# Fourteen seven-product pairs in rows in the last block, with weight sums made by adding transfers

## The chip, the cores and the metric

The program runs on one core of one Trainium2 chip. The metric is the device time of one launch in microseconds (us), as the median of several runs. The engines are TensorE (PE; PEld is its weight load), VectorE (DVE), ScalarE (ACT), GpSimd (POOL) and SyncE (SP), which issues the loads.

## What is computed

The reference chains a Mamba2 layer, a convolutional gated FFN, a differential attention layer, a second such FFN, and a mixed block that ends in a SwiGLU FFN, for 512 positions and a model width of 1024, all in float32. The change touches the code of the three FFNs; what matters most is the last one:

```
def swiglu(xn, w_gate, w_up, w_down):
    return (jax.nn.silu(xn @ w_gate) * (xn @ w_up)) @ w_down
...
D_FF = 2816        # 22 chunks of 128 features
```

The two FFNs before it have the same sizes, with a three-tap causal convolution between the product and the SiLU.

## The kernel before

**Layout.** Activations are kept feature-major: a chunk is 128 features on the partitions and 512 positions along the row. A float32 product is made of three passes of a rounded format (fp32r): each operand is split into a high part (ScalarE, a copy that rounds) and a low part (VectorE, a subtraction, called `cut`), and TensorE multiplies low by high, high by low and high by high.

**Plan.** A class `Plan` lays out the whole program ahead of time in ticks. A tick is one `Piece` of TensorE work: two chunks of contraction of a plain feature (6 matmuls of 512 columns) or one product of a seven-product pair (12 matmuls of 256 columns). Each engine's program then walks the ticks in order and issues what the plan has for that tick or for so many ticks earlier (`at("quad", T - age)`); real time is kept by semaphores alone, so an engine runs ahead until a wait holds it, and what stands behind the wait in its queue waits too.

**Weights.** They arrive by `load` on SyncE's queue into three raw buffers of 128x1024. A "unit" is one 128x1024 block (or less) that ScalarE splits and VectorE cuts into one of three high/low buffer pairs; `ring` schedules a unit's split two units ahead of its use and the cut `cut_age` ticks later. `load(r + 3)` waits until raw buffer `r` has been cut (and, for the pairs below, summed).

**The last FFN.** The gate and up features of chunk f (22 of each) share the input `n2`. A plain pair is two plain features: 48 matmuls of 512 columns in 8 ticks. Eleven of the 22 pairs (`QUADS` = 4, 5, 7, 8, 10, 12, 13, 15, 16, 18, 19) go by Strassen's scheme instead (`quad`): the 8 x 8 blocks (two halves of the positions, two halves of the contraction, gate and up) take seven products of 256 columns, 84 matmuls in 7 ticks. The products are formed in the order `PRODUCTS` in three banks, and their sums are finished from the banks by ScalarE copies and VectorE additions (`quads` in both programs). Sums of the inputs (`tees`) are made once. Sums of the weights are made per pair by VectorE from the two raw buffers: `sum1` and `sum2`, four additions of 128x512 into `s1` and `s2`. The gating product (`fmul`) of plain pairs runs on GpSimd, that of seven-product pairs on VectorE (`fmul_last`). No more than two such pairs stand in a row, and a plain pair stands between. `dn` are the down projections, after f = 11 and f = 21.

**Lines.** L1272 is every matmul, L1276 every transpose, L2230 VectorE's `tensor_tensor`, L2233 its `scalar_tensor_tensor`, L1715 ScalarE's copy, L1718 its other functions, L2877 GpSimd's `tensor_tensor`, L3027 the weight load on SyncE.

Of the kernel before, what the change touches and what calls it, by code (L numbers as in the profile page):

```python
# [9 lines left out]
F = mybir.dt.float32  # L10
# [143 lines left out]
QUADS = (4, 5, 7, 8, 10, 12, 13, 15, 16, 18, 19)  # L154
PRODUCTS = ("p1", "p2", "p6", "p5", "p7", "p3", "p4")
QUAD_BANK = {"p1": "b", "p2": "a", "p6": "b", "p5": "d", "p7": "b", "p3": "d", "p4": "b"}
QUAD_LAST = {"a": "p2", "d": "p3", "b": "p4"}
FIRST_ROW = 13
DIFF_ORDER = "k0 q0 k1 q1 v0 k2 q2 v1 k3 q3 k4 q4 v2 k5 q5 k6 q6 k7 q7 v3"


class Plan:
    def __init__(self):
        self.T = 0
        self.pieces = []
        self.units, self.unit_end, self.loads, self.quad_units = [], {}, [], {}
# [128 lines left out]
    def quad(self, f, gate, gate_c, up, up_c):  # L295

        key = ("gu", 2, f)
        self.until(lambda: self.past("tees", 3, 6) and self.place(
            [((*key, "b"), 0, 10), ((*key, "a"), 1, 4), ((*key, "d"), 3, 6)]), key)
        t = self.T  # L300
        self.loads += [(gate, 0, DC, gate_c + f * P, P), (up, 0, DC, up_c + f * P, P)]
        r = len(self.loads) - 2
        g = Group(key, False, "n2", 0, [], DC, 0, P, H2)
        sources = (("raw", r, 0, UNIT), ("s1", f, 0, UNIT), ("s2", f, 0, UNIT), ("raw", r + 1, S, S))
        for i, product in enumerate(PRODUCTS):
            if i % 2 == 0:
                age, self.cut_age = self.cut_age, 1 if i == 4 else self.cut_age
                u = self.ring(sources[i // 2])
                self.cut_age = age
                g.units.append(u)  # L310
            self.put(Piece(g, i // 2, i, i + 1, i == 0))
        self.quad_units[f] = (r, *g.units)
        for u, end in zip(g.units, (("bank", (*key, "a")), ("product", (f, "p5")), ("bank", (*key, "d")),
                                    ("bank", (*key, "b")))):
            self.unit_end[u] = end
        self.start("sum1", f, t - 5)
        self.start("sum2", f, t - 3)
        self.start("quad", f, t)
        src, i = h_of(2, f)
        self.lo[src, i] = t + 11  # L320
# [206 lines left out]
    def ffn(self, s, src, nxt, gate, gate_c, up, up_c, down, norm):  # L527
        late = 5 if s < 2 else 2
        if s == 2:
            for k in range(4):  # L530
                self.once("tees", k, lambda k=k: self.past("rms", "n2", 3) and (k == 0 or self.past("tees", k - 1, 4)))
        self.start("ffn", s)
        for h, (f0, nf) in enumerate(((0, 12), (12, 10))):
            def lo(h=h, f0=f0, nf=nf):
                for f in range(f0, f0 + nf):
                    t = self.ev.get(("up", s, f))
                    if t is not None:
                        self.lo[f"H{s}{h}", f - f0] = t + late

            self.rules.append(lo)  # L540
            for f in range(f0, f0 + nf):
                if s == 2 and f in QUADS:
                    self.quad(f, gate, gate_c, up, up_c)
# [285 lines left out]
class Waits:  # L829
# [23 lines left out]
    "tee_d", "tee_n1", "tee_t2", "tee_t", "tee_hi", "tee_lo", "sum1", "sum", "product", "q_copy", "q_row", "q_up", "q_read",  # L853
# [13 lines left out]
class Signals:  # L867
    def __init__(self, nc, ctx, known):
# [8 lines left out]
        self.tb2 = [Dma(sem(f"tb2{i}")) for i in range(4)]  # L877
        self.spill, self.mem, self.out = (Dma(sem(n)) for n in ("spill", "mem", "out"))
# [10 lines left out]
class Buffers:  # L889


    def __init__(self, nc, ctx):
# [41 lines left out]
        self.teeh, self.teel = (t[:, :, :].rearrange("p (i c) (h n) -> p i (c h) n", i=4, h=2) for t in (self.XBh, self.XBl))  # L934
# [29 lines left out]
    def ffn(self, st):  # L964
# [3 lines left out]
        self.fu = [sb(st, [P, S + 4]) for _ in range(3)]  # L968
        self.s1, self.s2 = sb(st, [P, UNIT]), sb(st, [P, UNIT])
# [91 lines left out]
class Kernel:  # L1061
# [34 lines left out]
    def gated(self, s, f):  # L1096

        return self.sig["fmul_last" if f in LAST_UP or (s == 2 and f in QUADS) else "fmul"].at(s, f)

    def source(self, u):  # L1100

        kind, r, at, n = self.plan.units[u]
        buf = self.buf.raws[r % N_W] if kind == "raw" else self.buf.s1 if kind == "s1" else self.buf.s2
        return buf[:, at:at + n]

    def source_ready(self, u):

        kind, r, _, _ = self.plan.units[u]
        return self.loaded(r) if kind == "raw" else self.sig["sum"].at(r, kind)
# [145 lines left out]
def tensor_program(eng, K):  # L1255
# [45 lines left out]
    def quads(p):  # L1301

        g, product = p.group, PRODUCTS[p.k0]
        f = g.key[2]
# [4 lines left out]
        u, half = g.units[p.k0 // 2], p.k0 % 2  # L1309
        wh, wl = (t[u % N_W][:, half * S:half * S + S].rearrange("p (k n) -> p k n", k=4) for t in (buf.his, buf.los))  # L1310
        w.wait_ge(*sig["cut"].at(u))
        if product == "p6":
            w.wait_ge(*sig["q_copy"].at(f, "p1"))
        elif product == "p7":
            w.wait_ge(*sig["q_copy"].at(f, "p6"))
        elif product == "p3":
            w.wait_ge(*sig["q_copy"].at(f, "p5"))
        elif product == "p4":
            w.wait_ge(*sig["q_read"].at(f))
        for k in range(4):  # L1320
            if product == "p1":
                xh, xl = (t[:, 0:H2] for t in buf.operand("n2", k))
                w.wait_ge(*K.ready("n2", k))
            elif product in ("p2", "p3"):
                xh, xl = (t[:, 0:H2] if product == "p2" else t[:, H2:S] for t in buf.operand("n2", 4 + k))
                w.wait_ge(*K.ready("n2", 4 + k))
            else:
                i = ("p5", "p6", "p7", "p4").index(product)
                xh, xl = buf.teeh[:, i, k, :], buf.teel[:, i, k, :]
                w.wait_ge(*sig["tee_lo"].at(k, i))  # L1330
# [3 lines left out]
        t.then_inc(*(fill(key) if QUAD_LAST[name] == product else sig["product"].up(f, product)))  # L1334
# [372 lines left out]

def scalar_program(eng, K):
# [11 lines left out]
    def split(u):  # L1720
        n = plan.units[u][3]
        w.wait_ge(*K.source_ready(u))
        if u >= N_W:
            w.wait_ge(*K.unit_done(u - N_W))
        copy(buf.his[u % N_W][:, 0:n], K.source(u)).then_inc(*sig["cut_hi"].up(u))

    def values(g):

        for j in range(g.n):
# [19 lines left out]
            if o == in_bank - 1:  # L1749
                t.then_inc(*leave(key))  # L1750

    ADDED = {"nf": ("out", 3), "nq": ("dn", 0, 1), "nf1": ("ao", 1), "nm": ("dn", 1, 1), "nx": ("mo",), "n2": ("xo", 1),
             "fin": ("dn", 2, 1)}
# [156 lines left out]
    def tees(T):  # L1910
        for k in at("tees", T):
            x_ready("n2", k)
            w.wait_ge(*full(("rs", "n2")))
            w.wait_ge(*sig.par.at())
            if k:
                for i in range(4):
                    w.wait_ge(*sig["tee_lo"].at(k - 1, i))
            copy(K.tee(0), buf.x[:, k, H2:S], pc("ffn2", k)).then_inc(*sig["tee_d"].up(k))
        for k in at("tees", T - 2):
            w.wait_ge(*full(("xo", 1, DC - 1)))  # L1920
            for i, sign in enumerate((1.0, -1.0, 1.0, -1.0)):
                w.wait_ge(*K.tee_ready(k, i))
# [1242 lines left out]
```

## Time and profile before

| | us |
|---|---|
| median of 3 runs | 2396.89 |
| lowest, highest | 2396.80, 2398.04 |
| profiled execution, its own time | 2399.27 |
| its span | 2397.5 |
| PE busy | 2371.2 |
| DVE busy | 1484.8 |
| ACT busy | 1086.1 |
| POOL busy | 357.9 |

The span is the stretch from the first to the last instruction; the profiled execution's own time has 1.8 us more around it, and lies 2.4 us above the median. The last FFN's gate and up part begins at about 2032 us of the span, its first seven-product pair at 2075.5 us, the rows end at 2309 us, and the down projection of the second half ends at about 2382 us.

### The profile page before, as it was taken

What the parts mean: (1) busy time and instruction counts of PE and PEld (TensorE: products, weight loads), DVE (VectorE), ACT (ScalarE), POOL (GpSimd) and SP (SyncE); (2) the same over time, 40 slices, a digit from 0 to 9 for tenths busy, and PEclk for the clock granted to TensorE, in tenths of its full rate; (3) what the DMA queues carried; (4) which work ended last, traced back from release to release, by engine and by line L of the source; (5) the groups of instructions that cost most, each with busy time, mean ns of one, the idle gap of its engine ahead of it and who ended that gap; (6) DMA issues with size and microseconds to landing.
All of it is one profiled execution on the core that took longest, in us unless ns stands there. A gap on an engine that the chain in (4) does not pass through costs nothing.

```text
span 2397.5 us, 30764 instructions
## 1 busy us (share of the span) xinstructions
PE 2371.2 (99%) x11952; PEld 1944.2 (81%) x11952; DVE 1484.8 (62%) x2356; ACT 1086.1 (45%) x1878; POOL 357.9 (15%) x286
## 2 busy tenths in 40 slices
PE   8999999999999999999999999999999999999999
PEld 6677878888888877788888877787788878898987
DVE  6778776763666777766456547534655445873763
ACT  6654554442445677644234334324443334442433
POOL 0252252210111000122011100001210001100001
PEclk9999999999999999999999999999999999999999
DMA  4532223223223221232332332231234332233232
GB/s 164 109 93 79 80 70 99 97 86 108 97 83 120 75 76 49 73 108 92 93 106 87 91 131 84 71 102 57 72 123 136 115 106 79 81 105 99 95 97 89
DMA packets 74847, 226.24 MB, mean 94 GB/s; under 512 B 8144, under 2 KB 12368, under 8 KB 74576
## 3 DMA queue, kind: packets, MB, share of 16 engines
q1 hardware_dynamic: 70272, 215.90, 28.1%
q10 hardware_dynamic: 4432, 8.39, 2.0%
q8 instruction: 95, 1.56, 0.3%
q14 instruction: 48, 0.39, 0.1%
HBM read 215.87 MB, written 8.39 MB: 94 GB/s over the span
## 4 chain that ended last, share of the span: by engine, by line
PE 60%; DVE 1%; ACT 0%; issue 0%; DMA 0%; POOL 0%; POOLq 0%; DVEq 0%; ACTq 0%; SPq 0%
PE bank L1272 59%; PE bank L1276 1%; DVE t L2230 1%; DVE t L2233 1%; ACT t L1715 0%; DVE t L2241 0%; DMA t<-in_w 0%; POOL t L2877 0%; ACT t L1718 0%; ACT L1718 0%; DVE t L2237 0%; DVE t L2798 0%; POOLq L3100 0%; DVEq L3100 0%; DVE t L2644 0%
## 5 line engine op out<-in xcount | busy, mean ns | idle before, releaser
L1272 PE MATMUL bank<-t 128*128 128x512 f32 (+5 forms) x11526 | 2346.4, 369 | 19.1 <-DVE t L2233 7.9
L1272 PEld LDWEIGHTS bank<-t 128*128 128x128 f32 (+2 forms) x11526 | 1901.0, 186 | 433.3 <-issue 80.1
L1715 ACT ACTIVATE t<-t 128x1024 fp32r<-128x1024 f32 (+5 forms) x676 | 564.0, 847 | 564.6 <-PE bank L1272 276.6
L2230 DVE TENSOR_TENSOR t<-t 128x1024 fp32r<-128x1024 f32 (+7 forms) x774 | 687.3, 901 | 202.9 <-ACT t L1715 192.4
L1718 ACT ACTIVATE t<-t 128x512 f32<-128x512 f32 (+6 forms) x610 | 367.5, 616 | 455.8 <-DVE t L2230 307.1
L2877 POOL TENSOR_TENSOR t<-t 128x512 f32<-128x512 f32 (+4 forms) x206 | 316.3, 1542 | 1551.9 <-ACT t L1718 559.7
L2230 DVE TENSOR_TENSOR t<-bank,t 128x512 f32<-128x512 f32 (+4 forms) x434 | 279.2, 648 | 425.2 <-PE bank L1272 414.7
L2233 DVE SCALAR_TENSOR_TENSOR t<-t 128x512 f32<-128x512 f32 (+5 forms) x536 | 386.6, 733 | 102.3 <-ACT t L1718 63.8
L1715 ACT ACTIVATE t<-bank 128x512 f32<-128x512 f32 (+4 forms) x184 | 84.7, 477 | 205.4 <-PE bank L1276 146.9
L2880 POOL TENSOR_SCALAR t<-t 128x128 f32<-128x128 f32 (+3 forms) x64 | 40.9, 645 | 478.6 <-ACT t L1715 247.6
L2233 DVE SCALAR_TENSOR_TENSOR t<-bank,t 128x512 f32<-128x512 f32 x56 | 38.5, 688 | 68.8 <-PE bank L1272 68.8
L1276 PE MATMUL bank<-t 128*128 128x128 f32 (+1 forms) x426 | 69.1, 277 | 1.9 <-ACT t L1715 1.2
L1718 ACT ACTIVATE t<-bank,t 128x128 f32<-128x128 f32 (+1 forms) x144 | 42.3, 392 | 44.9 <-DVE t L2798 39.2
L2233 DVE SCALAR_TENSOR_TENSOR t<-t,bank 128x512 f32<-128x512 f32 x40 | 28.4, 710 | 54.2 <-PE bank L1272 51.7
L2241 DVE CUSTOM_DVE_ANT_0 t<-bank,t 128x256 f32<-128x256 f32 (+3 forms) x128 | 55.7, 462 | 9.8 <-PE bank L1272 7.5
L1276 PEld LDWEIGHTS bank<-t 128*128 128x128 f32 (+1 forms) x426 | 50.0, 141 | 14.4 <-issue 4.2
L1718 ACT ACTIVATE t<-bank 128x512 f32<-128x512 f32 (+3 forms) x73 | 38.5, 539 | 13.4 <-PE bank L1272 8.5
L2237 DVE TENSOR_SCALAR t<-t 128x256 f32<-128x256 f32 (+6 forms) x88 | 33.6, 383 | 2.9
L1715 ACT ACTIVATE t<-bank,t 128x256 f32<-128x256 f32 (+1 forms) x32 | 15.3, 524 | 21.9 <-PE bank L1272 18.7
L1718 ACT ACTIVATION_READ_ACCUMULATOR t<-t 128x1 f32 x128 | 24.4, 191 | 0.0
L1718 ACT ACT_TABLE_LOAD x11 | 14.1, 1283 | 0.2
L2238 DVE TENSOR_SCALAR t<-bank 128x4 f32<-128x4 f32 (+1 forms) x14 | 2.2, 159 | 16.8 <-PE bank L1272 16.8
(30 smaller groups left out, 53.0 us busy)
## 6 DMA issues: line engine op xcount, KB each, us to landing
t<-in_w SPq DMA_DIRECT2D x304, 512.0 KB, 3.4
t<-in_w SPq DMA_DIRECT2D x48, 384.0 KB, 3.0
t<-in_w SPq DMA_DIRECT2D x56, 320.0 KB, 3.0
t<-in_w SPq DMA_DIRECT2D x28, 256.0 KB, 2.8
tab<-t ACTq DMA_DIRECT2D x1, 2560.0 KB
t<-in_x SPq DMA_DIRECT2D x8, 256.0 KB, 5.0
t<-tab SPq DMA_DIRECT2D x8, 256.0 KB, 3.7
spill<-t ACTq DMA_DIRECT2D x1, 2048.0 KB, 8.3
```

Of the source, the lines that this page charges most:

```text
L1272: return eng.matmul(out, lhs, rhs, start=start, stop=stop, skip_group_check=loose)
L1276: return eng.transpose(out, in_, ident[0:n, 0:n])
L1715: return eng.activation(out, in_, ACT.Copy, scale=scale)
L1718: return eng.activation(out, in_, f, bias=bias, scale=scale, accum_out=accum)
L2230: return eng.tensor_tensor(out, a, b, o)
L2233: return eng.scalar_tensor_tensor(out=out, in0=a, scalar=s, in1=b, op0=o0, op1=o1)
L2237: return eng.tensor_scalar(out, a, s0, None, o0)
L2238: return eng.tensor_scalar(out, a, s0, s1, o0, o1)
L2241: return eng.tensor_tensor_reduce(out, a, b, 1.0, FMAX, ADD, MIN, m)
L2877: return eng.tensor_tensor(out, a, b, o)
L2880: return eng.tensor_scalar(out, a, s, s1, o, o1)
```

## The change

In `QUADS` the last FFN gets fourteen pairs, 4, 7 to 10, 12 to 20, so that four and nine of them stand in a row; plain are 0 to 3, 5, 6, 11 and 21. The code can now serve the first two FFNs too, but their lists are empty. The products come in another order, and so do the weight parts. Of the four weight sums three are made by transfers: SyncE loads a base of 128x1536 into one of three sets (`base`, 19 ticks ahead of the pair); GpSimd issues a transfer of 128x1024 from memory that adds onto its first two thirds (`add1`, 14 ahead), and one of 128x512 that adds the first third onto the last (`add2`, 7 ahead). VectorE makes the fourth (`add3`, 3 ahead) into `sum4`. The sets are a buffer of its own, the memory of three norm buffers and that of the convolution's buffers. All gating products of the last FFN are now on VectorE. In the first two FFNs the steps behind a plain pair (except f = 11 and 21) come one to two ticks later (`ages`).

```diff
-QUADS = (4, 5, 7, 8, 10, 12, 13, 15, 16, 18, 19)
-PRODUCTS = ("p1", "p2", "p6", "p5", "p7", "p3", "p4")
+QUADS = {0: (), 1: (), 2: (4, 7, 8, 9, 10, 12, 13, 14, 15, 16, 17, 18, 19, 20)}
+SUM_AGES = ((26, 20, 12, 3), (26, 20, 12, 3), (19, 14, 7, 3))
+PRODUCTS = ("p1", "p5", "p6", "p3", "p7", "p2", "p4")
+QUAD_HALF = {"p1": (0, 0), "p5": (1, 0), "p6": (1, 1), "p7": (2, 0), "p3": (2, 1), "p4": (3, 0), "p2": (3, 1)}
+LAST_UP = (11, 21)
+def ages(s, f):
+    return (1, 0, 1, 2) if s == 2 else (3, 3, 4, 5) if f in LAST_UP else (4, 4, 6, 7)
+def on_vector(s, f):
+    return s == 2 or f in LAST_UP or f in QUADS[s]
...
-        sources = (("raw", r, 0, UNIT), ("s1", f, 0, UNIT), ("s2", f, 0, UNIT), ("raw", r + 1, S, S))
+        sources = (("raw", first, S), ("s12", (s, f), UNIT), ("s34", (s, f), UNIT), ("raw", last, UNIT))
...
-        self.start("sum1", f, t - 5)
-        self.start("sum2", f, t - 3)
+        for u in g.units[1:3]:
+            self.cut_at = {at: [v for v in units if v != u] for at, units in self.cut_at.items()}
+            self.cut_at.setdefault(next(at for at, units in self.split_at.items() if u in units) + 1, []).append(u)
+        for name, age in zip(("base", "add1", "add2", "add3"), SUM_AGES[s]):
+            self.start(name, (s, f), t - age)
...
-            tt(buf.s1[:, S:UNIT], b[:, 0:S], b[:, S:UNIT], ADD).then_inc(*sig["sum1"].up(f))
-            tt(buf.s1[:, 0:S], a[:, 0:S], buf.s1[:, S:UNIT], ADD).then_inc(*sig["sum"].up(f, "s1"))
-            tt(buf.s2[:, 0:S], a[:, 0:S], b[:, 0:S], ADD)
-            tt(buf.s2[:, S:UNIT], a[:, S:UNIT], buf.s1[:, 0:S], ADD).then_inc(*sig["sum"].up(f, "s2"))
+            w.wait_ge(*K.loaded(last))
+            w.wait_ge(*K.added(sf, 1))
+            tt(buf.sum4[:, :], K.sums(sf)[:, 2 * S:3 * S], buf.raws[last % N_W][:, S:UNIT], ADD).then_inc(*sig["sum"].up(sf))
...
+        for sf in at("add1", T):
+            w.wait_ge(*K.based(sf))
+            eng.dma_start(K.sums(sf)[:, 0:UNIT], K.region(region)[:, S:3 * S], accum_op=ADD).then_inc(
+        for sf in at("add2", T):
+            w.wait_ge(*K.added(sf, 0))
+            eng.dma_start(K.sums(sf)[:, 2 * S:3 * S], K.sums(sf)[:, 0:S], accum_op=ADD).then_inc(*sig.added[i][1].up())
...
+    def base(sf):
+        if before:
+            w.wait_ge(*sig["cut"].at(plan.quad_units[before][4]))
+        eng.dma_start(K.sums(sf)[:, 0:3 * S], K.region(region)[:, 0:3 * S]).then_inc(*sig.base[i].up())
```

**VectorE around the pair f = 19.** In the names t29 to t31 are raw buffers, t90 and t91 are `s1` and `s2`, t26 to t28 hold low parts. Before:

```order
L2230 TENSOR_TENSOR t90<-t31 128x512 [waits cut,w2,w1]
L2230 TENSOR_TENSOR t90<-t30,t90 128x512 [waits sum1]
L2230 TENSOR_TENSOR t81<-bank4,t81 128x256 [waits q_copy,full4]
L2230 TENSOR_TENSOR t80<-t86,t79 128x512 [waits hi]
L2230 TENSOR_TENSOR t27<-t91,t24 128x1024 [waits cut_hi]
L2230 TENSOR_TENSOR t91<-t30,t31 128x512 [waits cut]
L2230 TENSOR_TENSOR t91<-t30,t90 128x512 [waits sum]
L2230 TENSOR_TENSOR t28<-t29,t25 128x512 [waits cut_hi]
```

Now, in the row (t33, t85 and t86 are the three sets, t87 is `sum4`):

```order
L2319 TENSOR_TENSOR t26<-t29,t23 128x1024 [waits cut_hi]
L2319 TENSOR_TENSOR t79<-bank6,t79 128x256 [waits q_copy,full6]
L2319 TENSOR_TENSOR t87<-t86,t31 128x512 [waits cut,added01,w2]
L2319 TENSOR_TENSOR t80<-bank5,t80 128x256 [waits product]
L2319 TENSOR_TENSOR t27<-t30,t24 128x512 [waits cut_hi]
L2319 TENSOR_TENSOR t79<-bank3,t79 128x256 [waits full3]
L2319 TENSOR_TENSOR t79<-t79,t32 128x512 [waits empty6,empty3]
L2319 TENSOR_TENSOR t28<-t86,t25 128x1024 [waits cut_hi]
```

Four additions that waited for raw buffers have become one, which waits for the adding transfer (`added01`) as well, and it stands ahead of the addition that frees the bank of p7 for p4.

**GpSimd in the last FFN.** Before, it has the gating products (t<-t, 128x512):

```order
L2877 TENSOR_TENSOR t82<-t82,t81 128x512 [waits fsilu,empty1]
L2877 TENSOR_TENSOR t82<-t82,t81 128x512 [waits fsilu,empty0]
L2877 TENSOR_TENSOR t82<-t82,t81 128x512 [waits fsilu,empty2]
L2877 TENSOR_TENSOR t86<-t86,t85 128x512 [waits fsilu,empty2]
L2877 TENSOR_TENSOR t86<-t86,t85 128x512 [waits fsilu,empty1]
```

Now it has the adding transfers alone:

```order
L3119 DMA t85<-in_w 128x1024 [waits base2]
L3126 DMA t33<-t33 128x512 [waits added10,added11]
L3119 DMA t86<-in_w 128x1024 [waits base0]
L3126 DMA t85<-t85 128x512 [waits added20,added21]
L3119 DMA t33<-in_w 128x1024 [waits base1]
L3126 DMA t86<-t86 128x512 [waits added00,added01]
```

The second adding transfer of a pair stands behind the first one of the pair after it, and so behind that pair's base.

**SyncE ahead of the second row.** Before, the rows here are loads into the raw buffers alone; now bases stand between them:

```order
L3157 DMA t31<-in_w 128x1024 [waits cut]
L3171 DMA t33<-in_w 128x1536 [waits base1]
L3157 DMA t29<-in_w 128x512 [waits sum,cut]
L3171 DMA t85<-in_w 128x1536 [waits base2]
L3157 DMA t30<-in_w 128x1024 [waits cut]
```

A base goes out only when the raw load ahead of it in the queue has been let go.

## Rows read from the trace of the kernel before

**Rows 1.** The page, parts 1 and 5: busy time; costliest group of instructions.

```profile
PE 2371.2 (99%) x11952; PEld 1944.2 (81%) x11952; DVE 1484.8 (62%) x2356; ACT 1086.1 (45%) x1878; POOL 357.9 (15%) x286
...
L1272 PE MATMUL bank<-t 128*128 128x512 f32 (+5 forms) x11526 | 2346.4, 369 | 19.1 <-DVE t L2233 7.9
```

**Rows 2.** What PE waited for, 2022 to 2397 us: total, times, longest.

```profile
PE bank L1272 <- DVE t L2230: 1.7, 1, 1.7
PE bank L1276 <- ACT t L1715: 0.2, 1, 0.2
PE bank L1276 <- DVE t L2230: 0.2, 1, 0.2
```

**Rows 3.** PE's groups by form, 2108.66 to 2129.00 us (count, busy us, mean ns).

```profile
L1272 PE MATMUL bank<-t 128*128 128x256 f32 x168 | 20.5, 283 | 0.0
```

**Rows 4.** The same, 2149.98 to 2226.17 us.

```profile
L1272 PE MATMUL bank<-t 128*128 128x512 f32 x336 | 76.3, 389 | 0.0
```

**Rows 5.** Stretches: length; PE, PEld, DVE, ACT, POOL busy; clock; DMA share; GB/s.

```profile
2031.80:2075.50 43.70, 43.70 (x201) 36.27 (x200) 32.34 (x55) 20.97 (x39) 7.09 (x5) 1.00 0.24 80
2075.50:2097.80 22.30, 20.64 (x170) 20.28 (x169) 18.22 (x28) 10.50 (x17) 1.29 (x1) 1.00 0.29 97
2108.70:2129.00 20.30, 20.30 (x169) 20.16 (x168) 17.52 (x26) 9.84 (x16) 1.68 (x1) 1.00 0.26 81
```

**Rows 6.** The timeline, 2075 to 2084 us: start, us, instruction, idle before it.

```profile
2076.07 0.33 SPq L3027 DMA_DIRECT2D t<-in_w  x1
...
2079.51 1.42 DVE L2230 TENSOR_TENSOR t<-t 128x512 f32<-128x512 f32 x2 [1.25 <-DMA t<-in_w]
2079.67 1.58 ACT L1715 ACTIVATE t<-t 128x512 fp32r<-128x512 f32 x2 [2.17 <-POOL t L2877]
...
2081.19 3.15 DVE L2230 TENSOR_TENSOR t<-t 128x512 fp32r<-128x512 f32 x4
...
2083.06 1.21 PE L1272 MATMUL bank<-t 128*128 128x256 f32 x8 [1.67 <-DVE t L2230]
```

**Rows 7.** DVE's groups by form, 2108.7 to 2129 us.

```profile
L2230 DVE TENSOR_TENSOR t<-t 128x1024 fp32r<-128x1024 f32 x5 | 6.1, 1220 | 0.3 <-ACT t L1715 0.3
L2230 DVE TENSOR_TENSOR t<-bank,t 128x256 f32<-128x256 f32 x7 | 2.9, 420 | 1.4 <-PE bank L1272 1.4
L2230 DVE TENSOR_TENSOR t<-t 128x512 fp32r<-128x512 f32 x3 | 2.1, 684 | 0.4 <-ACT t L1715 0.4
```

**Rows 8.** ACT's groups by form, the same stretch.

```profile
L1715 ACT ACTIVATE t<-t 128x1024 fp32r<-128x1024 f32 x5 | 5.2, 1048 | 0.0
L1715 ACT ACTIVATE t<-t 128x512 fp32r<-128x512 f32 x4 | 2.5, 625 | 0.7 <-POOL t L2877 0.7
L1715 ACT ACTIVATE t<-bank 128x256 f32<-128x256 f32 x6 | 2.3, 384 | 6.8 <-PE bank L1272 6.8
```

**Rows 9.** The timeline of SyncE's queue, 2124 to 2127 us.

```profile
2125.10 0.33 SPq L3027 DMA_DIRECT2D t<-in_w  x1
```

**Rows 10.** The page, part 6: transfers, count, KB each, median us to landing.

```profile
t<-in_w SPq DMA_DIRECT2D x304, 512.0 KB, 3.4
...
t<-in_w SPq DMA_DIRECT2D x28, 256.0 KB, 2.8
...
spill<-t ACTq DMA_DIRECT2D x1, 2048.0 KB, 8.3
...
t<-in_mem ACTq DMA_DIRECT2D x1, 1024.0 KB, 5.6
```

**Rows 11.** The page, part 3: SyncE's DMA queue, its share of 16 engines.

```profile
q1 hardware_dynamic: 70272, 215.90, 28.1%
```

**Rows 12.** PE's groups by form in the first FFN, 320 to 790 us.

```profile
L1272 PE MATMUL bank<-t 128*128 128x512 f32 x2009 | 460.3, 390 | 0.0
```

More of the change, by code:

```diff
@@ L312, in quad @@
-        self.quad_units[f] = (r, *g.units)
-        for u, end in zip(g.units, (("bank", (*key, "a")), ("product", (f, "p5")), ("bank", (*key, "d")),
+        region = self.region((gate, 0, 4, gate_c + f * P, P), (up, 0, 4, up_c + f * P, P),
+                             (up, 4, 4, up_c + f * P, P), (gate, 4, 4, gate_c + f * P, P))
+        first = self.load(region, 0, S)
+        last = self.load(region, 2 * S, UNIT)
+        g = Group(key, False, FFN_IN[s], 0, [], DC, 0, P, H2)
+        sources = (("raw", first, S), ("s12", (s, f), UNIT), ("s34", (s, f), UNIT), ("raw", last, UNIT))
@@ L527, in ffn @@
     def ffn(self, s, src, nxt, gate, gate_c, up, up_c, down, norm):
[L528 to L531, printed above, removed]
+        apart = 4 if s == 2 else 12
+        for k in range(4 if QUADS[s] else 0):
+            self.once("tees", (s, k), lambda k=k: self.past("rms", src, 3) and (
+                k == 0 or self.past("tees", (s, k - 1), apart)))
         self.start("ffn", s)
@@ L967, in ffn @@
         self.fv = [sb(st, [P, S]) for _ in range(6)]
-        self.fu = [sb(st, [P, S + 4]) for _ in range(3)]
-        self.s1, self.s2 = sb(st, [P, UNIT]), sb(st, [P, UNIT])
+        self.fu_all = sb(st, [P, 3 * (S + 4)])
+        self.fu = [self.fu_all[:, i * (S + 4):(i + 1) * (S + 4)] for i in range(3)]
+        own = sb(st, [P, 3 * S])
+        self.sums = [[own, self.scratch], [own, self.scratch], [own, self.scratch, self.fu_all]]
+        self.sum4 = sb(st, [P, S])
     def diff(self, st):
@@ L1720, in split @@
     def split(u):
-        n = plan.units[u][3]
-        w.wait_ge(*K.source_ready(u))
+        for ready in K.source_ready(u):
+            w.wait_ge(*ready)
         if u >= N_W:
             w.wait_ge(*K.unit_done(u - N_W))
-        copy(buf.his[u % N_W][:, 0:n], K.source(u)).then_inc(*sig["cut_hi"].up(u))
+        for a, b, of in K.source(u):
+            t = copy(buf.his[u % N_W][:, a:b], of)
+        t.then_inc(*sig["cut_hi"].up(u))
     def values(g):
@@ L1916, in tees @@
                 for i in range(4):
[L1917 to L1920, printed above, removed]
+                    w.wait_ge(*sig["tee_lo"].at((s, k - 1), i))
+            copy(K.tee(0), buf.x[:, k, H2:S], pc(GAINS[src], k)).then_inc(*sig["tee_d"].up(sk))
+        for sk in at("tees", T - 2):
+            s, k = sk
+            teeh, _ = buf.tees[s]
+            w.wait_ge(*full((*ADDED[FFN_IN[s]], DC - 1)))
@@ L2185, in scalar_program @@
     for T in range(plan.T):
+        for u in plan.split_at.get(T, ()):
+            if 0 < u < len(plan.units) and plan.units[u][0] == "s34":
+                split(u)
         for g in at("ev", T):
@@ L2208, in scalar_program @@
         for u in plan.split_at.get(T - 1, ()):
-            if 0 < u < len(plan.units):
+            if 0 < u < len(plan.units) and plan.units[u][0] != "s34":
                 split(u)
@@ L2511, in quads @@
[L2511 to L2519 removed]
+        for s, f in at("quad", T - 4):
@@ L2835, in cut @@
     def cut(u):
-        n = plan.units[u][3]
         w.wait_ge(*sig["cut_hi"].at(u))
-        tt(buf.los[u % N_W][:, 0:n], K.source(u), buf.his[u % N_W][:, 0:n].bitcast(F), SUB).then_inc(*sig["cut"].up(u))
+        for a, b, of in K.source(u):
+            t = tt(buf.los[u % N_W][:, a:b], of, buf.his[u % N_W][:, a:b].bitcast(F), SUB)
+        t.then_inc(*sig["cut"].up(u))
     cut(0)
@@ L2865, in vector_program @@
                 cut(u)
-LAST_UP = (11, 21)
+        for sf in at("add3", T):
+            _, last, *_ = plan.quad_units[sf]
+            n = QUAD_LIST.index(sf)
+            w.wait_ge(*K.loaded(last))
+            w.wait_ge(*K.added(sf, 1))
+            if n:
+                w.wait_ge(*sig["cut"].at(plan.quad_units[QUAD_LIST[n - 1]][4]))
+            tt(buf.sum4[:, :], K.sums(sf)[:, 2 * S:3 * S], buf.raws[last % N_W][:, S:UNIT], ADD).then_inc(*sig["sum"].up(sf))
 def gpsimd_program(eng, K):
@@ L3042, in sync_program @@
                 load(plan.units[u][1] + N_W)
+        for sf in at("base", T):
+            base(sf)
         for h in at("tb", T):
```

432 lines of the change are left out of this document (261 added, 171 removed).

## The prediction

> **What bounds the kernel now.** I read the busy shares first: TensorE is busy 2371.2 of 2397.5 us and no other engine is above 62% [rows 1]. So the time is TensorE's own work plus its idle time, and an edit counts only by what it takes from either. Then its waits in the last part: from 2022 us to the end there is one wait worth naming, 1.7 us on VectorE [rows 2]. Then what its work costs there. In a stretch of two seven-product pairs 168 matmuls of 256 columns fill 20.34 us [rows 3], which is 121 ns each and 10.17 us for a pair of 84. In a stretch of plain work 336 matmuls of 512 columns fill 76.19 us [rows 4], 227 ns each and 10.89 us for a plain pair of 48. (The mean durations in these rows, 283 and 389 ns, overlap; the stretch divided by the count is the price.) The stretch of the first two seven-product pairs is 22.3 us long, that of the next two 20.3 [rows 5]: the 1.7 us of waiting lie in the first. The granted clock is 1.00, the 2.4 GHz level, in all of them.
>
> **Three more pairs of seven products.** Each saves 10.89 - 10.17 = 0.72 us of TensorE time: 3 x 0.72 = **2.2 us**. The plan gets three ticks shorter and no tick in it is empty, so none of this is given back by the plan itself; only a semaphore can do that.
>
> **The one wait.** At 2076.07 SyncE issues a raw load; VectorE idles for it until 2079.51, because the weight sums of f = 5 stand in its queue ahead of the cut that f = 4 needs; that cut ends at about 2083.0, and TensorE, idle for 1.67 us, starts again at 2083.06 [rows 6]. In the new order VectorE has no sum there that waits for a raw load of the next pair: f = 5 is plain, and the one sum left per pair waits for raw data loaded long before. I take the wait as gone: 1.67 us by the trace, 2.0 by the two stretches [rows 5], taken as **1.8 us**. What would be late next is the same cut behind `add3` of f = 4. Its transfers have no other pair's transfer in front of them, and 16 ticks (22 us) from base to sum, against 5.6 + 4.8 us for two transfers of about 1 MB and 768 KB below. I cost that at nothing.
>
> **VectorE and ScalarE per pair in a row.** Start to start, VectorE's operations take about 0.08 us less than their durations: 1.14 (1024 wide), 0.60 (512), 0.34 (256) [rows 7]. A pair needs 2 x 1.14 + 3 x 0.60 of cuts, 5 x 0.34 + 3 x 0.60 of finishing and 0.60 for `sum4`: 8.2 of 10.17 us. Before it had four sums, which makes 9.9 us, and only plain pairs between (less work each) paid that back; so rows of nine would not have gone then and can now. ScalarE needs 2 x 1.0 + 5 x 0.55 + 3 x 0.3 = 5.6 us [rows 8]. The tightest chain I find goes from the end of p4 of the pair before (0): split of the s34 unit in two copies to 1.4, SiLU to 2.0, gating product to 2.7, two cuts to 3.9; p3 wants it three ticks later, at 4.36 us. Slack 0.4 us. If it were missed by 0.2 us in each of 11 pairs that stand behind another, that is 2.2 us back; I take zero and keep 2.2 in the range. GpSimd loses the gating products of plain pairs (0.6 us more for VectorE per plain pair, in stretches where it has 32.3 of 43.7 us to do [rows 5]): hidden; uncovered it would be 8 x 0.6 us.
>
> **The adding transfers.** No row of before shows such a transfer, nor any issued by GpSimd. So bound it. Time runs from the start of pair n of a row; a tick is 10.17 / 7 = 1.45 us. SyncE's base for pair n+3 stands behind a raw load that waits for the cut of pair n's fourth unit. By the chain above (hi copy 4.0, split 5.0, cut 6.1) it goes out at about 6.4; in before the load behind such a cut went out at 2125.10 [rows 9], 6.3 us into its pair, which began at 2118.83 (one pair after 2108.66). 256 KB and the base of 768 KB go out together, 1 MB in all; 1 MB takes 5.6 us to land [rows 10], so the base is there at about **11.65**. Then GpSimd issues `add1` of pair n+3 (512 KB), and only then `add2` of pair n+2 (256 KB). VectorE's `sum4` for n+2 waits for that, and behind it in its queue stands the addition that frees the bank of p7 for p4 of pair n+1, which is due at 10.17 + 8.72 = 18.89. With 1.2 us for the two additions and the hand-over, `add2` must have landed by **17.7**. That leaves **6.05 us** for both transfers. Plain prices: 512 KB 3.4 us, and each further 256 KB (8.3 - 5.6) / 4 = 0.68 us [rows 10]. At the price of a plain copy 768 KB land in 4.1 us, 1.95 us early; if each byte costs double, like 1536 KB, in 6.1 us, just at the limit; if it costs threefold, like 2304 KB, in 8.1 us, 2.05 us late. A pair that is late makes the next one's time later too, and so gives the next transfer that slack: in a row every second pair pays. Places: f = 9 (and the first of its row, f = 7, whose base from f = 8 comes at the same distance), and 14, 16, 18: five. So the bounds are 0, 0.3 and **10 us**. Nothing excludes a small gain from this part, since sets are ready earlier than a stalled VectorE made them, but TensorE has no other wait to lose [rows 2]. I take 0, because the nearest rows are plain copies of the same sizes, and the limit is reached only at double price.
>
> A rule of the Trainium skill speaks against this: Collectives: The Full Stack, "The bandwidth ceiling", states that an adding transfer reads two sources for each write and ran at about half the rate of a copy. By that rule the price is the double one and the sum 0.3 us smaller, with no slack left. No row here can test it.
>
> **Throughput.** SyncE's queue moved 215.9 MB for 28.1% of the engines' time [rows 11]: 320 GB/s at full share. A pair in a row moves 1536 KB plainly (4.9 us of that) and 768 KB adding (2.5, 4.9 or 7.4 us): 7.4, 9.8 or 12.3 us of a 10.17 us pair. The third would bound the rows by itself: 2.1 us for each of 13 pairs, but the row above already holds part of it, and the share counts latency too.
>
> **The first two FFNs.** Their steps come one or two ticks later on ScalarE, VectorE and GpSimd. TensorE there fills 460.3 us with 2009 matmuls and no wait [rows 12]; the plan still finds every chunk ready when its down projection asks. Nothing gained, nothing lost.
>
> **The sum** against the profiled execution: 2399.27 - 2.2 - 1.8 = 2395.3. It lies 2.4 above the median of the runs, so the median should be 2396.89 - 4.0 = **2392.9 us**.
>
> **The rivals.** (a) In time, as above: 2391.5 to 2394.5. (b) Double price with some time for GpSimd to write the descriptors, say 0.5 us, or the short chain missed: 5 x 0.5 to 2.2 + 4 us given back: 2394.5 to 2401.7. For it: slack of 0.4 us on ScalarE's chain, none at double price. Against: every one of these pairs in before ran at 121 ns a matmul with VectorE at 17.5 of 20.3 us [rows 3, 5]. (c) Slower: the adding transfers cost threefold or more, `sum4` holds VectorE, and p4 of every second pair waits: 2392.9 + 10 = 2403 us. It decides from about 3.0 us of extra landing time: five places times 1.0 us eat the 4.0 us gained, and two more make it slower by 0.2%. For it: the reads of source and destination and the write of a byte are three passes; against: the transfer engines are at 26% in these stretches [rows 5]. (d) More gain than the sum: some of the 1.8 us beside it, or a start-up that goes better: under 2391.5.
>
> **How the numbers follow.** (a) 0.52, (b) 0.22, (c) 0.19, (d) 0.07. The likeliest is (a), 2392.9. The range 2391.0 to 2403.2 leaves out the lower half of (d) and the far part of (c). A measurement of this kernel can tell about 0.2% from no change, which is 4.8 us: below 2392.1 lie a fifth of (a) and (d), together 0.19; above 2401.7 lies (c), 0.19; between them 0.62.
>
> **What would show it.** The stretch of pairs 12 to 20 should be 9 x 10.17 = 91.5 us long with 756 matmuls and no wait; that of 7 to 10, 40.7 us. The first pair f = 4 should run in 10.2 us without the 1.7 us wait. VectorE should be at about 80% in the rows. SyncE's bases should go out 6.4 us into a pair and land 5 to 6 us later. The two adding transfers should land within 6 us of the base. It is wrong if TensorE's waits on VectorE's `tensor_tensor` in the rows add up to more than 2 us, if they come at p4 (transfers late) or at p3 (the short chain), or if waits appear in the first two FFNs.

## The result, and the profile after

| | before | after |
|---|---|---|
| median of the runs, us | 2396.85 | 2413.97 |
| span of the profiled execution | 2397.5 | 2413.3 |
| PE busy | 2371.2 | 2374.8 |

The change makes the kernel slower: 1.0066 times the time before, 95% interval 1.0054 to 1.0078, or 17 us where 4.0 us of gain were forecast. It lies outside the range as well. The differences in this document are all below 1% of the time; the interval beside each ratio says whether it is clear of the scatter.

TensorE's waits from 2022 us to the end, total, times and longest, are the middle line here and answer to [rows 2]; the lines around it are the waits of ScalarE and VectorE for the second adding transfer, from the same view of the kernel after:

```profile
ACT t L1782 <- DMA t<-t: 31.3, 7, 10.3
...
PE bank L1332 <- DVE t L2319: 13.5, 6, 4.5
...
DVE t L2319 <- DMA t<-t: 9.6, 1, 9.6
```

ScalarE waits for `t<-t`, the second adding transfer, seven times and 31.3 us in all; TensorE waits six times, 13.5 us. The first wait of each row shows in its timeline of TensorE (start, us, instruction, idle before it), here at the head of the second row:

```profile
2229.66 2.95 PE L1332 MATMUL bank<-t 128*128 128x512 f32 x18
2236.53 0.77 PE L1332 MATMUL bank<-t 128*128 128x256 f32 x2 [3.93 <-DVE t L2319]
```

The same at the head of the first row is 4.55 us. The stretches below, of the kernel after, have the columns of [rows 5]. The first three run from the start of the first head's wait to the end of the lower clock behind it; the others are behind the wait at the head of the second row, and around the start of pair 15:

```profile
2108.80:2112.00 3.20, 0.15 (x2) 0.00 (x0) 0.00 (x0) 0.96 (x1) 0.88 (x1) 1.00 1.00 180
2112.10:2113.50 1.40, 0.00 (x1) 0.03 (x1) 1.38 (x2) 0.00 (x0) 0.00 (x0) 0.50 1.02 195
2113.50:2118.90 5.40, 5.40 (x25) 5.40 (x26) 4.66 (x7) 3.29 (x6) 0.00 (x0) 0.50 0.17 31
...
2236.50:2241.80 5.30, 5.26 (x25) 5.30 (x26) 2.65 (x4) 1.33 (x2) 0.00 (x0) 0.50 0.75 141
2268.40:2269.10 0.70, 0.69 (x5) 0.69 (x6) 0.70 (x2) 0.00 (x0) 0.00 (x0) 1.00 0.87 363
2269.10:2272.50 3.40, 3.40 (x19) 3.40 (x18) 2.68 (x5) 1.63 (x3) 1.48 (x2) 0.50 0.60 201
```

Where the clock column is 0.50, TensorE is at the 1.2 GHz level. At the heads the clock fell while TensorE stood idle; behind the 2.0 us wait at 2268.4 it fell only when TensorE had worked again for 0.7 us. It stayed down for 5.4, 5.3 and 3.4 us in which TensorE worked, which costs half of that, 7.0 us. So a wait of this length costs more than itself.

The account of the span: the row of four takes 47.5 us and that of nine 104.65 us, where pairs without waits take 40.3 and 90.7 us (first experiment below). Together they lose 21.1 us: 13.5 of waiting, 7.0 of the lower level, and 0.6 of small change around them. Against that stands what the forecast counted as gain: 1.9 us at f = 4, whose 84 matmuls now take 10.07 us, 2.2 us for three pairs, and 1.3 us more than counted, since a pair takes 10.08 us and not 10.17. Net 21.1 - 5.4 = 15.7 us, and the spans differ by 15.8.

**Where the transfers stand.** The queues ahead of the second row, GpSimd first, then SyncE (start, us, instruction, idle before):

```profile
2223.34 0.88 POOL L3119 DMA_DIRECT2D t<-in_w  x1 [11.08 <-DMA t<-in_w]
2223.89 1.24 POOL L3126 DMA_DIRECT2D t<-t  x1
```

```profile
2217.21 0.42 SPq L3171 DMA_DIRECT2D t<-in_w  x1
2220.90 3.93 SPq L3157 DMA_DIRECT2D t<-in_w  x2
2224.87 0.48 SPq L3171 DMA_DIRECT2D t<-in_w  x1
```

GpSimd stood for 11.08 us until the base of f = 13, issued at 2217.21, had landed. Only then came `add1` of f = 13 and, half a microsecond behind it, `add2` of f = 12, whose own inputs had landed at about 2216.8, 7 us before. It landed at 2234.0, 10.1 us after its issue. Four transfers went out there within 1.6 us: these two, a raw load (the second of the pair of loads, at 2224.50) and the base of f = 14. VectorE and ScalarE waited 9.6 and 10.3 us for `add2`, and TensorE began p5 at 2236.53.

At a head it is ScalarE that counts. The second weight part (`s12` in the diff) contains the sum that `add2` makes, so its split waits for both transfers, and behind the split stand VectorE's cut and p5. Inside a row the wait comes at p4, by way of `sum4`, as the prediction has it.

The median landing times of the kernel after, by the DMA view (count, KB, us), against [rows 10]:

```profile
t<-in_w SPq DMA_DIRECT2D x14, 768.0 KB, 5.9
t<-in_w POOLq DMA_DIRECT2D x14, 512.0 KB, 5.5
t<-t POOLq DMA_DIRECT2D x14, 256.0 KB, 6.1
```

Inside the second row TensorE's matmul starts, counted in twelves, put the waits at p4 of pairs 14, 16, 17 and 18 (steps of 2.2, 1.0, 1.1 and 1.8 us from one start to the next, where a plain step is 0.12).

### The profile page after: what moved, and what is told of

The parts are those of the page before. It is cut to its first block, busy times and chain, and to the rows that moved or that the text cites. A ratio compares the mean times of both kernels' runs of the same rounds, so it can differ in the third digit from the quotient of the medians.

```text
span 2413.3 us, 31058 instructions
## 1 busy us (share of the span) xinstructions
PE 2374.8 (98%) x12060; PEld 1953.5 (81%) x12060; DVE 1476.1 (61%) x2367; ACT 1091.1 (45%) x1907; POOL 369.2 (15%) x305
## 3 DMA queue, kind: packets, MB, share of 16 engines
q0 software_dynamic: 4032, 11.01, 2.7%
## 4 chain that ended last, share of the span: by engine, by line
PE 56%; issue 4%; DMA 1%; DVE 1%; POOL 1%; ACT 0%; POOLq 0%; DVEq 0%; SPq 0%; ACTq 0%
PE bank L1332 55%; PE bank L1336 1%; DMA t<-in_w 1%; DMA t<-t 1%; DVE t L2319 0%; POOL t L3119 0%; ACT t L1782 0%; POOL t L3126 0%; DVE t L2322 0%; DVE t L2330 0%; DVE t L2326 0%; ACT t L1785 0%; DVE t L2905 0%; POOLq L3248 0%; POOL t L2990 0%
## 5 line engine op out<-in xcount | busy, mean ns | idle before, releaser
L1332 PE MATMUL bank<-t 128*128 128x512 f32 (+6 forms) x11634 | 2350.3, 368 | 31.3 <-DVE t L2319 14.5
L1332 PEld LDWEIGHTS bank<-t 128*128 128x128 f32 (+3 forms) x11634 | 1910.7, 187 | 440.0 <-issue 89.0
L2319 DVE TENSOR_TENSOR t<-t 128x1024 fp32r<-128x1024 f32 (+6 forms) x776 | 675.0, 890 | 228.8 <-ACT t L1782 195.4
L1782 ACT ACTIVATE t<-t 128x1024 fp32r<-128x1024 f32 (+6 forms) x696 | 567.2, 834 | 518.4 <-PE bank L1332 312.2
L2990 POOL TENSOR_TENSOR t<-t 128x512 f32<-128x512 f32 (+4 forms) x197 | 302.4, 1543 | 1310.7 <-ACT t L1785 577.2
L2322 DVE SCALAR_TENSOR_TENSOR t<-t 128x512 f32<-128x512 f32 (+5 forms) x539 | 387.0, 730 | 132.4 <-ACT t L1785 90.7
L1782 ACT ACTIVATE t<-bank 128x256 f32<-128x256 f32 (+4 forms) x193 | 88.0, 472 | 184.2 <-PE bank L1336 145.2
L3119 POOL DMA_DIRECT2D t<-in_w x14 | 12.5, 890 | 230.1 <-DMA t<-in_w 230.1
L3126 POOL DMA_DIRECT2D t<-t x14 | 15.8, 1131 | 17.3 <-DMA t<-in_w 17.3
```

Of the source, the lines that this page charges most:

```text
L1332: return eng.matmul(out, lhs, rhs, start=start, stop=stop, skip_group_check=loose)
L1782: return eng.activation(out, in_, ACT.Copy, scale=scale)
L2319: return eng.tensor_tensor(out, a, b, o)
L2322: return eng.scalar_tensor_tensor(out=out, in0=a, scalar=s, in1=b, op0=o0, op1=o1)
L2990: return eng.tensor_tensor(out, a, b, o)
L3119: eng.dma_start(K.sums(sf)[:, 0:UNIT], K.region(region)[:, S:3 * S], accum_op=ADD).then_inc(*sig.added[i][0].up())
```

## The experiments

All edits below are on the kernel after unless said otherwise.

**1. The second adding transfer one tick sooner.**

```diff
-SUM_AGES = ((26, 20, 12, 3), (26, 20, 12, 3), (19, 14, 7, 3))
+SUM_AGES = ((26, 20, 12, 3), (26, 20, 12, 3), (19, 14, 8, 3))
```

> Edit: the second adding transfer of a pair is issued 8 ticks ahead of it instead of 7, so that in GpSimd's queue it stands ahead of the first adding transfer of the next pair and no longer waits for that pair's base. Theory Q (queue order): the waits in the rows (about 17 us over the stall-free 2393) come from that place in the queue. Most of them go: 2393 to 2400. Theory P (price): the transfers take too long whatever their order, since adding costs double and several fly together. Then the waits only move to the first adding transfer: 2408 to 2416.

Measured 2392.38 us, 0.9977 of before (0.9968 to 0.9986). That is just below the range of theory Q. Not one wait of TensorE in the rows is left. GpSimd's queue in the plain stretch ahead of the first row and into it, with `t<-t` ahead of the next `t<-in_w` now:

```profile
2096.31 0.87 POOL L3126 DMA_DIRECT2D t<-t  x1 [7.23 <-DMA t<-in_w]
2099.51 0.88 POOL L3119 DMA_DIRECT2D t<-in_w  x1 [2.33 <-DMA t<-in_w]
```

In the kernel after the same pair of instructions stands the other way round, with `t<-t` of f = 7 at 2102.35:

```profile
2101.80 0.88 POOL L3119 DMA_DIRECT2D t<-in_w  x1 [10.64 <-DMA t<-in_w]
2102.35 1.24 POOL L3126 DMA_DIRECT2D t<-t  x1
```

TensorE's first matmul of f = 7 starts at 2105.26 in this run and at 2107.36 in the kernel after, so `add2` of f = 7 now goes out 9.0 us ahead of it and not 5.0. A tick is 1.44 us, so it is the new place that brings this, not the tick. In the kernel after both instructions belong to the same tick, and the order of two loops in `adds` puts `add1` first; changing places there should do the same, but was not run.

The price of the transfers hardly changed: the DMA view of this run has

```profile
t<-in_w SPq DMA_DIRECT2D x14, 768.0 KB, 6.4
t<-in_w POOLq DMA_DIRECT2D x14, 512.0 KB, 5.8
t<-t POOLq DMA_DIRECT2D x14, 256.0 KB, 5.7
```

and the stretches of its three groups of pairs (columns as in [rows 5]) are

```profile
2072.90:2083.00 10.10, 10.10 (x84) 9.98 (x84) 7.43 (x12) 5.79 (x9) 0.00 (x0) 1.00 0.17 52
2104.80:2145.10 40.30, 40.30 (x336) 40.21 (x335) 33.09 (x53) 22.72 (x39) 4.39 (x5) 1.00 0.60 151
2221.30:2312.10 90.80, 90.80 (x756) 90.71 (x755) 75.47 (x121) 50.44 (x88) 13.14 (x15) 1.00 0.77 199
```

The engines of the DMA are busy 77% here, more than the 69% of the same row in the kernel after, and TensorE is never idle. So with the transfers in this order neither their throughput nor the price of adding bounds the rows.

**2. Copies instead of additions.**

```diff
-            eng.dma_start(K.sums(sf)[:, 0:UNIT], K.region(region)[:, S:3 * S], accum_op=ADD).then_inc(
+            eng.dma_start(K.sums(sf)[:, 0:UNIT], K.region(region)[:, S:3 * S]).then_inc(
...
-            eng.dma_start(K.sums(sf)[:, 2 * S:3 * S], K.sums(sf)[:, 0:S], accum_op=ADD)
+            eng.dma_start(K.sums(sf)[:, 2 * S:3 * S], K.sums(sf)[:, 0:S])
```

> Leaves out the additions of the two transfers: they copy instead of adding (same sizes, same queue, same order), so the weight sums are wrong in value. Theory P: a copy moves a byte once, the landing of the 512 KB transfer falls from 5.5 us to about 4 and that of the 256 KB behind it from 6.1 to about 4.5; the rows lose most of their waits: 2393 to 2400. Theory Q: the second transfer still waits for the next pair's base in the queue, which lands as late: 2405 to 2412.

Measured 2397.91 us, 1.0002 of before (0.9993 to 1.0012). Landing times by its DMA view:

```profile
t<-in_w SPq DMA_DIRECT2D x14, 768.0 KB, 5.4
t<-in_w POOLq DMA_DIRECT2D x14, 512.0 KB, 4.2
t<-t POOLq DMA_DIRECT2D x14, 256.0 KB, 4.3
```

Adding costs 1.3 us more on the first transfer and 1.8 us on the second. The second goes out about 0.5 us behind the first, so from the issue of the first to the landing of both 4.8 us became 6.7. The time that the packets of GpSimd's queue took shows it more sharply. Packets, MB and share of the 16 engines' span, in the kernel after and then here:

```profile
q0 software_dynamic: 4032, 11.01, 2.7%
```

```profile
q0 software_dynamic: 3136, 11.01, 1.4%
```

Most of the loss is gone, so the price matters too, in the order as it stands. But 5.5 us against experiment 1 remain: a wait of 2.7 us and a low level of 3.4 us at the head of the first row, and two shorter waits in the second. The time lies in the range of theory P, while experiment 1 bore out theory Q. Taking away either the order or the price takes away most of the loss, so it takes both to make 17 us, and mending the order alone is enough.

**3. No adding transfers.** `adds` issues nothing, and what waited for them waits for the base.

```diff
-        for sf in at("add1", T):
+        for sf in ():
...
-        for sf in at("add2", T):
+        for sf in ():
```

> Leaves out the two adding transfers of every pair; what waited for them waits for the base alone. Everything else stays: rows, order on VectorE and ScalarE, bases, raw loads. Every theory that puts the loss on the adding transfers: no wait in the rows, 2392.5 to 2394.5, the stall-free sum. Rival V (the short chain on ScalarE and VectorE, or bases and raw loads alone): waits of 0.2 to 1 us per pair stay, 2396 or more.

Measured 2392.80 us (0.9979, 0.9970 to 0.9989), with no wait in the rows. The chain on ScalarE and VectorE and the bases and raw loads hold the pace by themselves, and experiment 1 is no slower than this: where they are in time, the adding transfers cost nothing that these medians can show.

**4. The kernel before, with rows.**

```diff
-QUADS = (4, 5, 7, 8, 10, 12, 13, 15, 16, 18, 19)
+QUADS = (4, 7, 8, 9, 10, 12, 13, 14, 15, 16, 17, 18, 19, 20)
```

> The kernel before, with the fourteen pairs of the kernel after in rows and nothing else changed: the four weight sums stay on VectorE. By my working VectorE then has 9.9 us of work for each pair of 10.17 us. Theory: rows cannot go without transfers; VectorE falls behind in its order of waits and TensorE waits 0.3 to 1.5 us at each of 11 pairs: 2398 to 2412. Rival: 9.9 is still below 10.17, the rows just fit, and three more pairs bring 2.2 us: 2394 to 2396.

Measured 2408.10 us (1.0041, 1.0026 to 1.0056). TensorE's waits from 2022 us on:

```profile
PE bank L1272 <- DVE t L2230: 9.5, 18, 1.2
DVE t L2230 <- DMA t<-in_w: 6.5, 8, 1.3
```

From the third to the eighth a pair in the long row takes 11.4 to 12.0 us, with two steps of 0.6 to 1.3 us in each where a plain one is 0.12. Over the long row (columns of [rows 5]):

```profile
2229.80:2330.50 100.70, 94.28 (x757) 91.41 (x756) 88.51 (x138) 48.37 (x79) 0.00 (x0) 1.00 0.28 88
```

VectorE is busy 88.5 us in nine pairs, 9.8 us a pair, against the 10.08 us in which TensorE could do one, so it has almost nothing with which to catch up after a wait. In this layout rows do need sums made elsewhere. Whether other loads or another order would let VectorE keep them was not tried, and the product order alone has no run of its own.

**5 and 6. The heads of the rows, and the rest.** In experiment 5 only `add2` of f = 7 and 12 is one tick sooner, in experiment 6 all but these two.

```diff
-            self.start(name, (s, f), t - age)
+            self.start(name, (s, f), t - age - (name == "add2" and f in (7, 12)))
```

```diff
-            self.start(name, (s, f), t - age)
+            self.start(name, (s, f), t - age - (name == "add2" and f not in (7, 12)))
```

> Edit on the kernel after: the second adding transfer of the first pair of each row (f = 7 and 12) alone is issued one tick earlier, ahead of the first adding transfer of the next pair; the others stay as they are. Theory: the loss at the head of the rows (4.6 and 3.9 us of waiting and about 5 us of TensorE at the 1.2 GHz level after it) is one place each, that inside the rows (5.6 us and 1.7 us of the lower level) comes from the others. So 2414 - 13 = about 2400. Rival: with the heads in time the pairs inside the rows come sooner and wait more, as each late pair gave the next one slack: 2404 to 2410.

> The complement: every second adding transfer is one tick earlier except those of f = 7 and 12. Theory: both heads keep their wait of about 4 us and the lower level after it, the insides have none: 2392.5 + 8.5 + 4 to 5 = 2405 to 2406. Rival: the heads wait because the whole chain of transfers is late, so they are better too: below 2400.

Measured 2406.68 us (1.0035, 1.0023 to 1.0047) and 2406.30 us (1.0031, 1.0021 to 1.0041). TensorE's waits on VectorE from 2022 us on, of experiment 5 and then 6:

```profile
PE bank L1332 <- DVE t L2319: 9.7, 7, 3.6
```

```profile
PE bank L1332 <- DVE t L2319: 9.0, 2, 4.6
```

Experiment 6 is as worked out: two waits at the heads (at p5 of f = 7 and 12), the clock at the lower level for 6.8 us around the end of each, and 13.9 us above experiment 1. Experiment 5 went as its rival had it. The second row had no head wait, but six waits inside, 6.1 us where there were 5.0. In the first row a wait of 3.6 us came at p4 of f = 7, for `sum4` of f = 8, with the lower level around it. GpSimd there:

```profile
2099.67 0.88 POOL L3119 DMA_DIRECT2D t<-in_w  x1 [4.12 <-DMA t<-in_w]
2108.84 0.88 POOL L3119 DMA_DIRECT2D t<-in_w  x1 [8.29 <-DMA t<-in_w]
2110.63 0.88 POOL L3126 DMA_DIRECT2D t<-t  x1 [0.91 <-DMA t<-in_w]
```

`add1` of f = 8, issued at 2099.67, took 10.7 us to land; `add2` had to wait for that, whatever its place, and then took 6.5 us beside `add1` of f = 9, issued ahead of it. So this one wait is slow landing and place together. The repetition of experiment 1 (experiment 12 below) shows the difference that the place makes: there the same `add1` took 10.1 us, but `add2` went out ahead of `add1` of f = 9 and landed in 3.3 us. VectorE waited for it, and TensorE did not:

```profile
2112.43 0.69 DVE L2319 TENSOR_TENSOR t<-t 128x512 f32<-128x512 f32 x1 [0.88 <-DMA t<-t]
```

By these rows p4 of f = 7 had about 0.3 us in hand there, an estimate: the better order has no large reserve at the first head.

**7. The gating products back on GpSimd**, on the kernel of experiment 1.

```diff
-    return s == 2 or f in LAST_UP or f in QUADS[s]
+    return f in LAST_UP or f in QUADS[s]
```

> On the kernel of the first experiment (second adding transfers one tick earlier): the gating products of plain pairs of the last block go back to GpSimd. Theory: GpSimd's queue now holds adding transfers that wait for bases, so the gating product of f = 5 or 6 waits behind them, and the high and low parts of that chunk are late; but the down projection asks for them much later. TensorE waits nowhere or up to 2 us before f = 7 to 9: 2392.4 to 2395. Rival: the product held up blocks ScalarE's queue (its high part stands ahead of splits): 2396 to 2402.

Measured 2397.08 us (0.9992, 0.9982 to 1.0001), 4.7 above experiment 1. GpSimd's queue, and then ScalarE:

```profile
2105.06 0.86 POOL L3126 DMA_DIRECT2D t<-t  x1 [4.82 <-DMA t<-in_w]
2108.82 0.87 POOL L3119 DMA_DIRECT2D t<-in_w  x1 [2.90 <-DMA t<-in_w]
2109.40 1.59 POOL L2990 TENSOR_TENSOR t<-t 128x512 f32<-128x512 f32 x1
```

```profile
2111.02 0.63 ACT L1782 ACTIVATE t<-t 128x512 fp32r<-128x512 f32 x1 [3.51 <-POOL t L2990]
2111.55 0.37 ACT L1782 ACTIVATE t<-bank 128x256 f32<-128x256 f32 x1
```

A gating product stood behind two transfers that waited for their predecessors. ScalarE's high part waited 3.5 us for it and held up the copy from the bank behind it, for which p3 of f = 7 waits; TensorE stood for 2.1 us and its clock was down for 3.4 us. An earlier wait of ScalarE for such a product, 6.6 us long, held up nothing on TensorE. The rival holds: products that stand behind waiting transfers in GpSimd's queue cost 4.7 us here.

**8. Eleven pairs, new sums**, on the kernel of experiment 1.

```diff
-QUADS = {0: (), 1: (), 2: (4, 7, 8, 9, 10, 12, 13, 14, 15, 16, 17, 18, 19, 20)}
+QUADS = {0: (), 1: (), 2: (4, 7, 8, 10, 12, 13, 15, 16, 18, 19, 20)}
```

> On the kernel of the first experiment: only eleven pairs (4, 7, 8, 10, 12, 13, 15, 16, 18, 19, 20), with sums by transfers. It separates the three added pairs from the rest. Theory: the 1.8 us wait at f = 4 is gone without them and a pair runs in 10.08 us instead of 10.17, so 2.4 us slower than the first experiment with fourteen (three times 0.81): 2394.8. Rival: all of the gain is from the added pairs: 2396.9.

Measured 2396.26 us (0.9992, 0.9982 to 1.0001), between the two expectations. The profile has no wait in the rows and every pair at 10.08 us. From the start of f = 4 to the end of f = 20 it is 2.5 us longer than experiment 1 and 2.9 shorter than before, by the starts of the matmuls; the median gives only 0.6 to 1.6 us of gain against before. Medians of these kernels scatter by about 1 us, so the medians do not settle it; the profile agrees with the 2.4 us worked out for three pairs.

**9. Bases two ticks sooner.**

```diff
-SUM_AGES = ((26, 20, 12, 3), (26, 20, 12, 3), (19, 14, 7, 3))
+SUM_AGES = ((26, 20, 12, 3), (26, 20, 12, 3), (21, 14, 7, 3))
```

> On the kernel after: every base is asked for 21 ticks ahead of its pair instead of 19, which puts it ahead of a raw load in SyncE's queue; in a row it then waits for the cut of the s34 unit (3.9 us into a pair by my working) and not for that of the fourth unit (6.4 us). The adding transfers keep their order. Theory: the late step is the landing of a base behind which GpSimd's queue stands, so bases 2.5 us sooner remove the waits inside the rows (0.9 to 2.1 us each) and shorten those at the heads by 2 to 3 us each: 2394 to 2400. Rival: the landing itself stretches when three or four transfers fly together, and sooner bases only collide with other loads: 2405 to 2414.

Measured 2402.99 us (1.0018, 1.0008 to 1.0027), between the two. TensorE waits 4.4 us for VectorE where it waited 13.5, and its clock is down once, for 3.4 us, so sooner bases do help. But the landing stretched, by its DMA view:

```profile
t<-in_w SPq DMA_DIRECT2D x14, 768.0 KB, 6.2
t<-in_w POOLq DMA_DIRECT2D x14, 512.0 KB, 5.8
t<-t POOLq DMA_DIRECT2D x14, 256.0 KB, 7.4
```

Both theories have a part; asking sooner mends less than asking in the right order.

**10 to 12. Fifteen pairs, the old ages, and experiment 1 again**, all on the kernel of experiment 1.

```diff
-QUADS = {0: (), 1: (), 2: (4, 7, 8, 9, 10, 12, 13, 14, 15, 16, 17, 18, 19, 20)}
+QUADS = {0: (), 1: (), 2: (4, 6, 7, 8, 9, 10, 12, 13, 14, 15, 16, 17, 18, 19, 20)}
```

```diff
-    return (1, 0, 1, 2) if s == 2 else (3, 3, 4, 5) if f in LAST_UP else (4, 4, 6, 7)
+    return (1, 0, 1, 2) if s == 2 else (3, 3, 4, 5)
```

> On the kernel of the first experiment (second adding transfers one tick earlier): a fifteenth pair, f = 6, so that the first row is 6 to 10. Theory: every pair saves 10.89 - 10.08 = 0.81 us and the row's head has the same distances: 0.8 us below the run of the first experiment in this call, 2391.6. Rival: the base of f = 6 and 7 come while the input sums are still being made, the head waits again and the TensorE clock falls: 2396 to 2402.

> On the kernel of the first experiment: in the first two FFNs the steps behind a plain pair come as soon as in the kernel before (3, 3, 4, 5 for all). Theory: TensorE never waits there in either, so no difference to the first experiment's kernel, within 0.5 us. Rival: the later steps made room, and without them 1 us or more comes back.

> The kernel of the first experiment once more, as the base of comparison for the others of this call: 2392.4 within 1 us, and clear of the kernel before by 0.1 to 0.3%.

Measured 2391.95 us (0.9974, 0.9963 to 0.9984), 2392.59 us (0.9979, 0.9970 to 0.9988) and 2392.14 us (0.9973, 0.9963 to 0.9983). The repetition stands: one number in the plan turns 17 us of loss into about 5 us of gain. The old ages in the first two FFNs make no difference, as expected. The fifteenth pair runs without a wait (five pairs in 50.4 us), and its profiled span is 1.2 us shorter, but the medians do not tell the two apart; both beat the kernel before and the kernel after.

## Why the prediction was wrong

**What bounds the kernel**: right, and it explains much of the loss: every us in which TensorE stood idle came back in full, and the lower clock on top.

**Three pairs, and the wait at f = 4**: right. A pair without waits takes 10.08 us, 0.09 less than I took from [rows 3], where the second of two pairs still had small waits. The stall-free sum was 4.0 us, and the kernels that reach it (experiments 1, 3 and 12) are 4.8 to 5.4 us faster than the medians of before beside them.

**The engines' work and the short chain**: right. No wait came at p3, and experiment 4 bore out that in this layout VectorE could not have kept the four sums.

**The adding transfers**, a term that was set at zero, is the step that failed. Its mechanism, `add2` behind the next pair's base and first transfer, was right; what was put into it was not. The rows gave back 21.1 us where the term had 0 and its upper bound 10. In the long row the base went out 6.6 us into a pair (forecast 6.4), 7.4 in pair 15. It took 5.0 to 6.8 us to land (forecast 5.25), 0.3 us passed until GpSimd's issue, and both adding transfers took another 6.5 to 7.1 us (forecast 4.1 at the plain price that the sum used, 6.1 at the double one). The waits inside the row came at p4, as foreseen. Each term was short, and `add2` landed 19.3 to 20.3 us into the pair where 17.7 was the limit: 1.6 to 2.6 us late, with no slack to spend. I had taken zero because the nearest rows were plain copies "and the limit is reached only at double price". Experiment 2 gives that price: the additions add 1.9 us to the pair of transfers, against 2.0 for the double price, and the same 11.01 MB took 2.7% of the transfer engines' time instead of 1.4%. The double price stood among my own bounds, and I took the lower one. The Trainium skill, Collectives: The Full Stack, "The bandwidth ceiling", states for the reducing step of a ring collective that it reads two sources for each write and ran at about half the rate of a copy. The engines' time here agrees; the landing of one 512 KB transfer does not double, it went from 4.2 to 5.5 us.

**"At the same distance"** is the second error. For the head of the first row I took the window of the row's inside, and f = 12, the head of the second, was not among my five places at all. At each head four transfers start within 1.6 to 2.2 us, and the landing of `add2` took 8.6 and 10.1 us. The wait came at p5, behind ScalarE's split of the second weight part, a path that my working did not have. These two places cost 8.5 us of waiting and 5.3 us of the lower level, two thirds of the loss. That all `add2` stand behind the next pair's base I had written down, but only to work out a window; the obvious question, what if it stood one place further ahead, was not asked.

**The clock** was in no term. A wait of about 4 us brought 5.3 to 5.4 us of TensorE work at 1.2 GHz, 2.7 us more for each head. "In a row every second pair pays" was wrong too: 14, 16, 17 and 18 paid, and 9 did not.

**The first two FFNs**: right. From 229 to 2022 us TensorE waits 4.9 us before and 4.8 after, and experiment 11 found no difference.

**The rivals**: (c) named the mechanism and p4 for the inside of the rows, but at 0.19 and with 2403 us as its end. A likelihood near a half would have been fair, since at the double price the window of 6.05 us was already overrun, by 6.1. The prices under (b), 2.5 to 6.2 us given back, make 2395.4 to 2399.1 us, not the 2394.5 to 2401.7 written there; the likeliest value does not hang on it. **Throughput** was no bound: the DMA engines ran at 77% in the row without waits.

## What to carry to other kernels

In a queue that issues in order, as GpSimd's does here, a transfer whose inputs are ready must not stand behind one that still waits; go through each pair of neighbours in the queue and ask which is needed first, before you work out how long anything takes. Where a window is worked out to have no slack, take the upper price and the crowded landing time, and add what TensorE's clock costs after the wait. An age in a plan that only shifts a wait by one tick can decide the order of two instructions, and here that, not the tick, was its effect.

## What the runs showed of the hardware

Transfers issued by GpSimd had not been seen in this kernel. Issuing one took 0.88 us on GpSimd, or 1.24 for the second of two close together, and 0.54 us for one that only copies. A 512 KB transfer that adds landed in 5.5 us where the copy of the same size and queue took 4.2. The queue moved the same bytes in 4032 packets when adding and in 3136 when copying. An adding transfer of 256 KB that was alone landed in about 3.2 us and took up to 10.1 us beside others, so how many are in flight mattered more than the price of adding.

In the last FFN, after waits of 3.6 to 4.6 us the granted clock was at 1.2 GHz for 6.8 us, of which TensorE worked 4.8 to 5.5 us (the kernel after, experiments 5 and 6). After waits of 2.0 to 2.7 us it was there for 3.4 us, and fell only when TensorE had worked again for 0.3 to 1.2 us (the kernel after, experiments 2, 7 and 9). After the waits up to 1.7 us in these runs and before, it stayed at 2.4 GHz.
